# Moving the first-product weights of an MLP to another place in SBUF

## The chip, the cores and the metric

The kernel runs on one core of a Trainium2 chip. The metric is the device time of one execution in microseconds (us), as the median of several runs. The core has a matrix engine (TensorE, PE in the profile, with its weight loads under PEld), VectorE (DVE), ScalarE (ACT), GpSimd (POOL) and SyncE (SP, which here issues DMAs). Its on-chip memory SBUF has 128 partitions; every tensor there has a start, given below in bytes of a partition.

## The reference

Two transformer layers run on 1024 tokens of width 1024 and, in the first layer, 256 context tokens as well. Everything is float32. Each layer modulates its input, runs an attention mixer (the first layer's has a spatial-gating branch beside it), adds, normalises, and then runs the MLP:

```python
x = _layer_norm(ALPHA * x + g_m * _squared_relu_mlp(x * (1 + sc_m) + sh_m, mlp_w1[l], mlp_w2[l]), ...)

def _squared_relu_mlp(h, w1, w2):          # h: tokens x 1024, w1: 1024 x 4096, w2: 4096 x 1024
    return jnp.square(jax.nn.relu(h @ w1)) @ w2
```

The first layer's MLP has 1280 rows (tokens and context), the second's 1024.

## The kernel before

The program is a chain of stages (the list at the end of `build`), each a block of five engine programs. Engines meet at the end of a block, and inside one they are ordered only by semaphores written out by hand. No planner or allocator chooses anything: the order of the instructions is the source's, and every SBUF tensor is placed at an explicit start. `Place` hands out starts one behind the other.

Precision is kept by splitting each float32 operand into a high and a low part (names that end in `h` and `l`), each of a type that TensorE takes as it is. Each product is then three matmuls: high by high, high by low, low by high. The call is `pe.matmul(out, weights, streamed)`: the second argument is loaded into the array (a LDWEIGHTS in the trace), the third is streamed past it. In the profile's names, `pair<-hth,m_wah` streams `hth` past the weights `m_wah`.

`hth` and `htl` are the modulated columns: the layer's input, turned so that features lie on partitions, with 1280 tokens for each of 8 feature tiles. They start at byte 20608 and end at byte 102528, called `after_ht`. Before the change the sums `y` (10 tiles of 1024 elements) start there, `moments` lie behind them, and `after_y` is 143584. The MLP stage and the row stages of kind 2 place all their tensors from `after_y`; the other stages place theirs from `after_ht`, over `y`.

`stage_mlp` (L1251 to L1438) goes over the 4096 hidden features in NCH = 16 steps of 256, that is M = 2 tiles of 128. For each step:

- SP loads `rawa` (a piece of w1) and `rawb` (a piece of w2).
- ACT copies `rawa` to `wah` (L1323) and POOL subtracts to get `wal` (L1346), two tiles of 128x1024 each; ACT and DVE do the same for `wbh` and `wbl`.
- PE runs the first product (L1434 to L1436) for each group of 512 tokens (the first layer has a third group of 256), for each of the two hidden tiles and 8 feature tiles, three matmuls each: 48 matmuls for a group. The weights are `wah` and `wal`; the streamed operands are `hth` and `htl`.
- ACT takes the relu and the square to `ath`, POOL squares to `sq`, and DVE subtracts to get `atl`.
- PE runs the second product (L1418 to L1420) of the step before, 12 matmuls for each tile of 128 tokens, with weights `ath` and `atl` and streamed `wbh` and `wbl`. It stands ahead of the first product of the same group, so runs of the two products alternate.
- DVE adds the result to `y` (L1368).

The attention stage has a projection loop, `job` (L1163 to L1165), with the same triple in the same form: the same `hth` and `htl`, in the same groups of 512 and 256 tokens and the same 8 feature tiles, past the weights `a_wkh`, `a_wqh`, `a_wvh` and their low parts. It also differs in the start of the weights, the PSUM banks used, the number of feature tiles run without a break, and what runs around it. The gating stage (L709 to L711) has the roles turned: its weights are `hth` and `htl`, and it streams `gate_wh` and `gate_wl`.

Starts before the change, in bytes, with the remainder after division by 128 (worked out from the source):

| tensors | role | start | remainder |
|---|---|---|---|
| hth, htl | streamed in the first product | 20608, 61568 | 0 |
| m_wah, m_wal | weights of the first product | 143584, 151776 | 96 |
| m_wbh, m_wbl | streamed in the second product | 159968, 168160 | 96 |
| m_ath, m_atl (layer 0; 1) | weights of the second product | 192736, 202976; 192736, 200928 | 96 |
| a_wkh, a_wqh, a_wvh | weights in attention | 114816, 118912, 123008 | 0 |
| a_wkl, a_wql, a_wvl | weights in attention | 127104, 131200, 135296 | 0 |
| gate_wh, gate_wl | streamed in the gating stage | 102528, 135296 | 0 |
| y, moments | DVE's sums | 102528, 143488 | 0 |

All steps inside these tensors are multiples of 128 bytes.

Of the kernel before, what the change touches and what calls it, by code (L numbers as in the profile page):

```python
# [13 lines left out]
F32 = mybir.dt.float32  # L14
F32R = mybir.dt.float32r
# [4 lines left out]
P = 128  # L20
D = 1024
KT = D // P
SEQ, CTX = 1024, 256
TOK = SEQ + CTX
XT, CT = SEQ // P, CTX // P
# [3 lines left out]
FC = 256  # L29
# [1222 lines left out]
def stage_mlp(nc, io, k, layer):  # L1252
# [6 lines left out]
    tag = f"m{layer}"  # L1259
    sb = Place(nc, tag, k.after_y)  # L1260
    tiles = XT + CT if layer == 0 else XT
    groups = groups_of(tiles * P)
    NG, M = len(groups), FC // P
    J = NG * M
    NB1 = 3 if J % 3 == 0 else 4
    wah, wal = sb("wah", [P, M, KT, P], F32R), sb("wal", [P, M, KT, P], F32R)
    wbh, wbl = sb("wbh", [P, M, D], F32R), sb("wbl", [P, M, D], F32R)
    rawa, rawb = sb("rawa", [P, M, KT, P]), sb("rawb", [P, M, D])
    ath, atl = sb("ath", [P, M, tiles * P], F32R), sb("atl", [P, M, tiles * P], F32R)
# [197 lines left out]
def build(nc, io, out):  # L1467
    k = Kept(nc)
    k.out = out
    at = 16512  # L1470
    small = {}
    for name, shape in (("ident", [P, P]), ("eps", [P, 1]), ("mod", [P, 2, 48, 2])):
        small[name] = nc.alloc_sbuf_tensor_at(f"kept_{name}", shape, F32, offset=at)
        at += (int(np.prod(shape[1:])) * 4 + 31) // 32 * 32
    assert at <= BASE
    k.ident, k.eps, k.mod = (small[x] for x in ("ident", "eps", "mod"))
    k.hth = nc.alloc_sbuf_tensor_at("hth", [P, KT, TOK], F32R, offset=BASE)
    k.htl = nc.alloc_sbuf_tensor_at("htl", [P, KT, TOK], F32R, offset=BASE + KT * TOK * 4)
    k.after_ht = BASE + 2 * KT * TOK * 4
    k.y = nc.alloc_sbuf_tensor_at("y", [P, XT + CT, D], F32, offset=k.after_ht)  # L1480
    k.mv = nc.alloc_sbuf_tensor_at("moments", [P, XT + CT, 2], F32, offset=k.after_ht + (XT + CT) * D * 4)
    k.after_y = k.after_ht + (XT + CT) * D * 4 + 96
    assert (XT + CT) * 2 * 4 <= 96
    pairs = [nc.alloc_psum_tensor(f"pair{i}", [P, 1024], F32) for i in range(4)]
    k.pair = pairs
    k.bank = [pairs[i // 2][:, (i % 2) * 512:(i % 2) * 512 + 512] for i in range(8)]
    k.x_dram = nc.dram_tensor("x_rows", [TOK, D], F32, kind="Internal").ap()
    k.cat_dram = nc.dram_tensor("cat_cols", [D, TOK], F32, kind="Internal").ap()
    k.gate_dram = nc.dram_tensor("gate_rows", [2, 2, 2 * KT, P], F32, kind="Internal").ap()
    k.skew_dram = nc.dram_tensor("skewed_rpb", [16, P, GRID_R * RP_W], F32, kind="Internal").ap()  # L1490
    k.rp_dram = nc.dram_tensor("padded_rpb", [16, RP_W, RP_W], F32, kind="Internal").ap()
    stages = [(stage_modulation, ()), (stage_rows, (0, 0)), (stage_attention, (0,)), (stage_gating, ()), (stage_rows, (0, 1)),
              (stage_mlp, (0,)), (stage_rows, (0, 2)),
              (stage_attention, (1,)), (stage_rows, (1, 1)), (stage_mlp, (1,)), (stage_rows, (1, 2))]
    for stage, args in stages:
        stage(nc, io, k, *args)
        k.end_stage()
# [22 lines left out]
```

## Time and profile before

| | us |
|---|---|
| median of 3 runs | 3334.58 (3331.59 to 3334.59) |
| profiled execution, its own time | 3334.39 |
| its span, first to last instruction | 3332.6 |
| PE busy in the span | 2858.8 (86%) |
| MLP of layer 0, first matmul to last run's end | 875.85 to 1770.99 |
| MLP of layer 1 | 2567.08 to 3279.92 |

The profile records one execution. A matmul's recorded duration overlaps the next one's, since they are pipelined, so what a matmul costs is the distance from its start to the start of the next. The timeline gives starts to 0.01 us; over a run of n matmuls the distance is the difference of two starts divided by n. PEclk is the granted TensorE clock as a share of 2.4 GHz.

### The profile page before, as it was taken

To read this page: it belongs to the slowest core of one execution; us is meant where nothing else is said; L and a number is where in the kernel's file an instruction comes from. 1 tells how busy PE (TensorE), PEld (TensorE's weight loads), DVE (VectorE), ACT (ScalarE), POOL (GpSimd) and SP (SyncE) were. 2 spreads that over 40 slices of the span, in tenths; PEclk is the share of its full clock that TensorE was granted. 3 is DMA by queue.
4 is the path that set the end of the run, shared out by engine and by line. 5 is a ranking of instruction groups with operands and counts; after the bars stand their busy time and mean duration, and the time that the engine had idled before them with its cause. 6 is when DMAs were issued, how large, how long until landed. Compare 5 with 4: busy or idle time off the path is not lost. (4 is left out here: it accounts for less than half of the span.)

```text
span 3332.6 us, 40345 instructions
## 1 busy us (share of the span) xinstructions
PE 2858.8 (86%) x15572; PEld 2328.3 (70%) x15572; DVE 1392.0 (42%) x2191; ACT 886.1 (27%) x1664; POOL 557.6 (17%) x377
## 2 busy tenths in 40 slices
PE   3477776869799999999994799999877999999993
PEld 0166665748588888888883688888665888888882
DVE  1156563136433333333338355555554333333336
ACT  0133333324312121212113344334333221122111
POOL 0000000113312121212126100000013222221124
PEclk8778788979899999999996899999988999999997
DMA  9721002034201010101013211110053111111114
GB/s 366 284 81 29 21 21 72 19 120 133 85 29 47 29 48 27 49 27 49 27 38 114 81 45 39 33 45 20 7 171 101 51 50 50 50 44 44 50 38 114
DMA packets 201373, 228.92 MB, mean 69 GB/s; under 512 B 15000, under 2 KB 148720, under 8 KB 201264
## 3 DMA queue, kind: packets, MB, share of 16 engines
q1 hardware_dynamic: 200800, 227.19, 21.8%
q8 instruction: 74, 1.21, 0.1%
q14 instruction: 35, 0.29, 0.0%
q10 hardware_dynamic: 464, 0.23, 0.0%
HBM read 198.98 MB, written 32.63 MB: 70 GB/s over the span
## 5 line engine op out<-in xcount | busy, mean ns | idle before, releaser
L1434 PE MATMUL pair<-hth,m_wah 128*128 128x512 f32 (+1 forms) x1280 | 480.1, 375 | 27.8 <-POOL m_wal L1346 27.8
L1368 DVE TENSOR_TENSOR y<-y,pair 128x1024 f32<-128x1024 f32 x288 | 351.2, 1220 | 337.4 <-PE pair L1420 337.2
L1435 PE MATMUL pair<-htl,m_wah 128*128 128x512 f32 (+1 forms) x1280 | 480.0, 375 | 0.0
L1436 PE MATMUL pair<-hth,m_wal 128*128 128x512 f32 (+1 forms) x1280 | 479.5, 375 | 0.0
L1418 PE MATMUL pair<-m_wbh,m_ath 128*128 128x512 f32 x1152 | 449.2, 390 | 4.6 <-DVE y L1368 4.6
L1420 PE MATMUL pair<-m_wbh,m_atl 128*128 128x512 f32 x1152 | 449.5, 390 | 0.0
L1419 PE MATMUL pair<-m_wbl,m_ath 128*128 128x512 f32 x1152 | 449.4, 390 | 0.0
L1396 DVE TENSOR_TENSOR m_atl<-m_sq,m_ath 128x512 fp32r<-128x512 f32 x160 | 102.2, 639 | 715.5 <-POOL m_sq L1353 715.5
L1336 ACT ACTIVATE m_rel<-pair 128x512 f32<-128x512 f32 x160 | 88.7, 554 | 1037.2 <-PE pair L1436 1037.2
L1353 POOL TENSOR_TENSOR m_sq<-m_rel 128x512 f32<-128x512 f32 x160 | 154.5, 965 | 1231.3 <-ACT m_rel L1336 1231.3
L1434 PEld LDWEIGHTS pair<-hth,m_wah 128*128 128x128 f32 x1280 | 242.4, 189 | 76.1 <-POOL m_wal L1346 28.6
L1436 PEld LDWEIGHTS pair<-hth,m_wal 128*128 128x128 f32 x1280 | 242.5, 189 | 47.4
L1435 PEld LDWEIGHTS pair<-htl,m_wah 128*128 128x128 f32 x1280 | 242.2, 189 | 47.3
L1418 PEld LDWEIGHTS pair<-m_wbh,m_ath 128*128 128x128 f32 x1152 | 216.3, 188 | 53.4 <-DVE y L1368 7.6
L1419 PEld LDWEIGHTS pair<-m_wbl,m_ath 128*128 128x128 f32 x1152 | 216.2, 188 | 46.1
L1420 PEld LDWEIGHTS pair<-m_wbh,m_atl 128*128 128x128 f32 x1152 | 216.2, 188 | 45.5
L982 ACT ACTIVATE a_sx<-a_sx,a_small 128x640 f32<-128x640 f32 (+4 forms) x208 | 160.8, 774 | 179.6 <-DVE a_small L1084 179.6
L1218 PE MATMUL pair<-a_ptt,a_v 128*64 128x128 f32 x1888 | 138.3, 296 | 72.6 <-ACT a_ptt L989 68.7
L1218 PEld LDWEIGHTS pair<-a_ptt,a_v 128*64 128x64 f32 x1888 | 111.2, 146 | 103.1 <-ACT a_ptt L989 81.9
L1346 POOL TENSOR_TENSOR m_wal<-m_rawa,m_wah 128x1024 fp32r<-128x1024 f32 x64 | 152.6, 2406 | 49.8 <-ACT m_wah L1323 49.8
L381 ACT ACTIVATE r_modt<-pair,kept_mod 128x128 f32<-128x128 f32 x304 | 109.1, 529 | 183.4 <-PE pair L523 171.4
L538 PE MATMUL pair<-r_wh,r_cath 128*128 128x512 f32 x288 | 117.7, 409 | 38.9 <-DVE r_wl L443 22.6
(171 smaller groups left out, 4460.6 us busy)
## 6 DMA issues: line engine op xcount, KB each, us to landing
mod_w<-in_w_mod SPq DMA_DIRECT2D x24, 2048.0 KB, 20.0
m_rawa<-in_mlp_w SPq DMA_DIRECT2D x64, 512.0 KB, 4.2
m_rawb<-in_mlp_w SPq DMA_DIRECT2D x64, 512.0 KB, 4.2
x_rows<-r_res SPq DMA_DIRECT2D x28, 512.0 KB, 3.1
r_raw<-cat_cols SPq DMA_DIRECT2D x18, 512.0 KB, 5.9
m_rawa<-x_rows SPq DMA_DIRECT2D x18, 512.0 KB, 3.8
r_xin<-in_x SPq DMA_DIRECT2D x16, 512.0 KB, 3.9
skewed_rpb<-padded_rpb SPq DMA_DIRECT2D x8, 512.0 KB, 6.4
```

The costliest lines, as they stand in the source:

```text
L538: pe.matmul(o, cath[:, t % 2, kt, :], wh[:, kt, n], start=kt == 0, stop=False)
L982: act.activation(x, x, ACT.Exp, bias=sm[:, 0:1], scale=-1.0, accum_out=sm[:, 1:2]).then_inc(s_exp, 1)
L1218: i = pe.matmul(TA[ds, 0:P], v[:, it % KB, kt, ds], ptt[:, hh, j, :], start=j == 0, stop=j == len(tiles) - 1)
L1346: pool.tensor_tensor(wal[:, m, :, :], rawa[:, m, :, :], f32(wah[:, m, :, :]), ALU.subtract).then_inc(s_alow, 1)
L1353: pool.tensor_tensor(sq[:, m % 2, 0:n], r, r, ALU.mult).then_inc(s_sq, 1)
L1368: dve.tensor_tensor(k.y[:, t, :], k.y[:, t, :], k.pair[t % 2][:, :], ALU.add).then_inc(s_y, 1)
L1418: pe.matmul(o, ath[:, m, ts], wbh[:, m, cols], start=m == 0, stop=False)
L1419: pe.matmul(o, ath[:, m, ts], wbl[:, m, cols], start=False, stop=False)
L1420: i = pe.matmul(o, atl[:, m, ts], wbh[:, m, cols], start=False, stop=m == M - 1)
L1434: pe.matmul(o, wah[:, m, kt, :], xh, start=kt == 0, stop=False)
L1435: pe.matmul(o, wah[:, m, kt, :], xl, start=False, stop=False)
L1436: i = pe.matmul(o, wal[:, m, kt, :], xh, start=False, stop=kt == KT - 1)
```

## The change

`wah` and `wal` are placed from `after_ht`, directly behind `htl`, by a placer of their own. `y` and `moments` start 16 KB (16384 bytes) further on, behind them, and so does everything that is placed from `after_y`. In the MLP stage the two tensors that left that sequence were 16 KB together, so all other MLP tensors keep their starts. The row stages of kind 2 move their tensors by 16 KB. No instruction, loop, wait or transfer is added, removed or put in another place.

```diff
@@ stage_mlp
-    wah, wal = sb("wah", [P, M, KT, P], F32R), sb("wal", [P, M, KT, P], F32R)
+    near = Place(nc, f"{tag}n", k.after_ht)
+    wah, wal = near("wah", [P, M, KT, P], F32R), near("wal", [P, M, KT, P], F32R)
+    assert near.at <= k.y_at
     wbh, wbl = sb("wbh", [P, M, D], F32R), sb("wbl", [P, M, D], F32R)
@@ build
     k.after_ht = BASE + 2 * KT * TOK * 4
-    k.y = nc.alloc_sbuf_tensor_at("y", [P, XT + CT, D], F32, offset=k.after_ht)
-    k.mv = nc.alloc_sbuf_tensor_at("moments", [P, XT + CT, 2], F32, offset=k.after_ht + (XT + CT) * D * 4)
-    k.after_y = k.after_ht + (XT + CT) * D * 4 + 96
+    k.y_at = k.after_ht + 2 * FC * KT * 4
+    k.y = nc.alloc_sbuf_tensor_at("y", [P, XT + CT, D], F32, offset=k.y_at)
+    k.mv = nc.alloc_sbuf_tensor_at("moments", [P, XT + CT, 2], F32, offset=k.y_at + (XT + CT) * D * 4)
+    k.after_y = k.y_at + (XT + CT) * D * 4 + 96
```

| tensors | start before | start after | remainder by 128 before, after |
|---|---|---|---|
| m_wah, m_wal | 143584, 151776 | 102528, 110720 | 96, 0 |
| y, moments | 102528, 143488 | 118912, 159872 | 0, 0 |
| row stages of kind 2, first tensor | 143584 | 159968 | 96, 96 |
| other MLP tensors | 159968 and on | the same | 96, 96 |

## Rows read from the trace of the kernel before

**Rows 1.** The page: the span, and PE's busy time, share and instructions.

```profile
span 3332.6 us, 40345 instructions
PE 2858.8 (86%) x15572; PEld 2328.3 (70%) x15572; DVE 1392.0 (42%) x2191; ACT 886.1 (27%) x1664; POOL 557.6 (17%) x377
```

**Rows 2.** Busy time by stretch: the two MLP stages; the first line names the columns.

```profile
core 0: us, PE busy (x) PEld busy (x) DVE busy (x) ACT busy (x) POOL busy (x), PEclk, DMA share, GB/s
875.85:1770.99 895.14, 892.02 (x4223) 742.38 (x4224) 307.16 (x317) 166.28 (x254) 185.66 (x135) 1.00 0.13 41
2567.08:3279.92 712.84, 711.34 (x3069) 578.46 (x3070) 246.17 (x240) 139.31 (x190) 157.53 (x101) 1.00 0.17 49
```

**Rows 3.** Waits of PE (us in total, times, longest), windows 870:1740 and 2600:3290.

```profile
PE pair L1434 <- POOL m_wal L1346: 13.4, 1, 13.4
PE pair L1418 <- DVE y L1368: 1.5, 2, 0.8
```

**Rows 4.** Groups by line and form: busy us, mean ns of one, idle before.

```profile
L1418 PE MATMUL pair<-m_wbh,m_ath 128*128 128x512 f32 x1152 | 449.2, 390 | 4.6 <-DVE y L1368 4.6
L1434 PE MATMUL pair<-hth,m_wah 128*128 128x512 f32 x1024 | 408.3, 399 | 27.8 <-POOL m_wal L1346 27.8
...
L1346 POOL TENSOR_TENSOR m_wal<-m_rawa,m_wah 128x1024 fp32r<-128x1024 f32 x64 | 152.6, 2406 | 49.8 <-ACT m_wah L1323 49.8
...
L1434 PE MATMUL pair<-hth,m_wah 128*128 128x256 f32 x256 | 71.9, 281 | 0.0
```

**Rows 5.** PE's timeline, layer 0's MLP: start us, duration us, instruction.

```profile
1106.49 0.40 PE L1434 MATMUL pair<-hth,m_wah 128*128 128x512 f32 x1
...
1117.73 0.39 PE L1418 MATMUL pair<-m_wbh,m_ath 128*128 128x512 f32 x1
...
1119.82 0.39 PE L1418 MATMUL pair<-m_wbh,m_ath 128*128 128x512 f32 x1
...
1123.22 0.28 PE L1434 MATMUL pair<-hth,m_wah 128*128 128x256 f32 x1
...
1128.92 0.40 PE L1418 MATMUL pair<-m_wbh,m_ath 128*128 128x512 f32 x1
...
1129.62 0.39 PE L1418 MATMUL pair<-m_wbh,m_ath 128*128 128x512 f32 x1
...
1139.82 0.40 PE L1434 MATMUL pair<-hth,m_wah 128*128 128x512 f32 x1
```

**Rows 6.** The same view, layer 1's MLP.

```profile
2779.96 0.40 PE L1434 MATMUL pair<-hth,m_wah 128*128 128x512 f32 x1
...
2791.20 0.39 PE L1418 MATMUL pair<-m_wbh,m_ath 128*128 128x512 f32 x1
```

**Rows 7.** The same view, layer 0's attention projections.

```profile
208.08 0.28 PE L1163 MATMUL pair<-hth,a_wkh 128*128 128x256 f32 x1
...
210.96 0.40 PE L1163 MATMUL pair<-hth,a_wqh 128*128 128x512 f32 x1
...
212.12 0.39 PE L1165 MATMUL pair<-hth,a_wql 128*128 128x512 f32 x1
...
230.20 0.39 PE L1163 MATMUL pair<-hth,a_wvh 128*128 128x512 f32 x1
...
235.64 0.28 PE L1163 MATMUL pair<-hth,a_wvh 128*128 128x256 f32 x1
```

**Rows 8.** The same view, the gating stage.

```profile
549.65 0.39 PE L709 MATMUL pair<-gate_wh,hth 128*128 128x512 f32 x1
...
550.33 0.39 PE L709 MATMUL pair<-gate_wh,hth 128*128 128x512 f32 x1
```

**Rows 9.** The same view, the start of layer 0's MLP.

```profile
881.14 0.63 PE L1434 MATMUL pair<-hth,m_wah 128*128 128x512 f32 x1
881.57 0.63 PE L1435 MATMUL pair<-htl,m_wah 128*128 128x512 f32 x1
```

**Rows 10.** The instructions that use y: duration min/median/max in ns.

```profile
L1368 DVE TENSOR_TENSOR y<-y,pair x288: 1172/1221/1223, 909.9 to 3284.1; 128x1024 f32<-128x1024 f32 x144
```

## The prediction

> **What bounds the kernel now.** I read the page first: the span is 3332.6 us and PE is busy for 86% of it [rows 1]. The busy time by stretch then shows where PE is the limit. In the two MLP stages it is busy for 892.02 of 895.14 us and 711.34 of 712.84 us, at the full granted clock, while DVE, POOL and ACT are busy for about a third of the time or less [rows 2]. The waits confirm it: in nearly all of layer 0's MLP PE waits once, 13.4 us for the first step's m_wal, and in layer 1's it waits 1.5 us for y [rows 3]. So these 1608 us, almost half of the span, last as long as PE's instructions take one after another. What a matmul costs there reaches the end of the kernel whole.
>
> The groups by form give the first hint: a 512-column matmul of the first product is recorded with 399 ns, one of the second product with 390 ns [rows 4]. Durations overlap, so I went to the timeline and divided differences of starts.
>
> - First product, layer 0: 48 matmuls from 1106.49 to 1117.73 us, 11.24 / 48 = 234.2 ns each [rows 5].
> - First product, layer 1: 48 from 2779.96 to 2791.20, again 234.2 ns [rows 6].
> - Second product: 45 from 1129.62 to 1139.82, 10.20 / 45 = 226.7 ns [rows 5].
> - Attention projections: 24 from 230.20 to 235.64, 5.44 / 24 = 226.7 ns [rows 7].
> - Gating: 3 from 549.65 to 550.33, 226.7 ns [rows 8].
>
> So the first product's matmuls, 47% of the 512-column ones in the MLP, cost 7.5 ns more than the others, with the same number of columns and at the same clock. The reader should see that the attention projection is the same triple over the same hth and htl with the same groups and feature tiles. It runs at 226.7. Of the differences between the two loops the source leaves the weights' place, the PSUM bank and the neighbours. Other PE work runs before and after both, and the second product, which shares the MLP's neighbours, is quick.
>
> **What the place could have to do with it.** No row gives an address, so this is inference from the source's starts. It is not distance and not a region: hth's and htl's feature tiles begin up to 122,976 bytes ahead of m_wah and end 41,056 ahead of it, and attention's weights begin 12,288 to 114,688 bytes behind them, an overlapping stretch, and the gating stage streams gate_wl through the very bytes in which m_wah and m_wal lie, at 226.7 [rows 8]. What separates the slow pair from every fast pair is the remainder by 128: weights at 96 and streamed operand at 0, where attention and gating have 0 and 0 and the second product has 96 and 96. After the change the first product has 0 and 0, and its weights lie in the area in which attention's do. That they would then behave as attention's is my forecast.
>
> **Term 1, the 512-column matmuls of the first product.** There are 16 steps x 2 groups x 2 hidden tiles x 8 feature tiles x 3 = 1536 per layer, 3072 in all; the form's count of 1024 for one of the three lines agrees [rows 4]. At the start of each MLP stage the granted clock is low for some dozen matmuls and the distance there is 0.43 us (881.14 to 881.57), which is 512 columns at 1.2 GHz with nothing on top [rows 9]. I leave 24 of them out: 3048 x 7.5 ns = 22.9 us. All of it is on the path.
>
> **Term 2, the switches between the products.** After a run of the first product the second takes nine matmuls to settle: 1117.73 to 1119.82 is 2.09 us where nine at 226.7 would be 2.04 [rows 5]. Attention's five matmuls after its switch from 256 to 512 columns take 1.16 us instead of 1.13 [rows 7]. There are 64 switches from a 512-column run into the second product (2 groups x 16 steps x 2 layers). If both runs keep one beat these 0.05 us vanish, -3.2 us. If instead each switch into the first product gains such a tail too, since one operand family is at remainder 0 and the other at 96, it is +3.2 us. No row shows a switch between two quick pairs of different remainders, so both stay as bounds; I take 0, the middle, since nothing is nearer to either.
>
> **Term 3, the 256-column matmuls.** In the MLP 48 take 1123.22 to 1128.92, 118.8 ns each [rows 5]; in attention 24 take 208.08 to 210.96, 120.0 ns [rows 7]. Here the present place is the better one. There are 3 x 256 = 768 [rows 4]: 768 x 1.2 = +0.9 us.
>
> **Term 4, y and the rest.** y's start keeps remainder 0 and the row stages' tensors keep 96. The 288 additions into y, which lie in up to ten different places, take 1172 to 1223 ns with a median of 1221 [rows 10], so a place 16 KB further on has no price that this view shows. In the loop each addition is also hidden by the 12 matmuls of the next tile (12 x 0.227 = 2.72 us against 1.22); without that cover it would cost PE the difference to 2.72. At the ends of the stages, where it is not hidden, the whole spread over 18 tiles is 18 x 0.05 = 0.9 us either way. I take 0. Writing wah and wal is ACT's and POOL's work, 2.4 us for a tile on POOL [rows 4]. It starts when a step's first product ends and is wanted after 48 matmuls of the second (10.9 us): two tiles and ACT's copies fit. If the cover were gone PE would wait as at the first step [rows 3]. SP's queue and all transfers are as before, and rawa does not move.
>
> **A rule that speaks against it.** The Trainium skill, SBUF — State Buffer, "Who interferes with whom", gives PE two SBUF read ports, one for the streamed operand and one for weights, calls them independent, and says that PE never waits on anyone. By it the weights' place could not matter, and the sum would be 0. The trace shows 234.2 against 226.7 for the same triple [rows 5 to 7], which that rule leaves unexplained; no row shows the cause.
>
> **Sum.** -22.9 + 0 + 0.9 + 0 = -22.0 us. The profiled execution took 3334.4 us, 1.8 more than its span, and this lies around the instructions and stays. That gives 3312.4; the median of the runs is 3334.6, 0.2 higher, so 3312.6.
>
> **Rivals.**
>
> 1. *Nothing changes* (12%). The 7.5 ns come from something other than the place: the banks, the neighbours, or how the loop is fed. The page's independent ports say the same. For it: only one slow pair exists in the trace, and no view names a cause. Against it: attention's loop issues the same instructions over the same columns at 226.7 [rows 7], and the second product has the same neighbours at 226.7 [rows 5]. Time: 3334.6.
>
> 2. *Only one of the two weight tensors becomes quick* (6%). wah feeds two matmuls of each triple and wal one. If the distance from the streamed rows matters as well as the remainder, one of them could stay slow. For: they lie 8 KB apart. Against: hth's and htl's different distances make no difference today. Gain a third or two thirds of 22.9, less 0.9: 3334.6 - 6.7 = 3327.9 or 3334.6 - 14.4 = 3320.2.
>
> 3. *Both products become slow* (3%). The second product today finds its beat again within nine matmuls after each switch. With two quick families of different remainders it may lose it at each switch, and the first may not gain it. The price would be 3456 x 7.5 = +25.9 us on the second product (3 x 1152 [rows 4]) with term 1 gone: 3360. It decides against the change once the mean distance over all 6504 of them is above today's (3048 x 234.2 + 3456 x 227.7) / 6504 = 230.7 ns, where 227.7 is the second product with its tail, (2.09 + 39 x 0.2267) / 48 us. Against: attention's switches settle in five matmuls [rows 7].
>
> **How the numbers follow.** My forecast has 79%. Its own range is the bounds of terms 2 and 4 (4.1 us) and the runs' scatter of up to 3 us below the median: 3306 to 3318. The range for 8 in 10 reaches into the second rival: 3306 to 3328; no change and slower (15%) and a few per cent of the rest stay out. What a measurement can tell from no change is about 0.2%, 6.7 us, so faster means below 3327.9. Faster: 79 + 5 = 84%. Same: 12 + 1 = 13%. Slower: 3%.
>
> **What would show it.** In the timeline after, 48 matmuls of the first product should take 10.88 us instead of 11.24, and a 256-column run 5.76 instead of 5.70. L1434's mean at 512 columns should fall from 399 to about 391 ns, and L1418's should stay near 390. PE's waits should stay as they are, and the two MLP stages should shrink by about 11 us each (layer 0 some 0.9 less, for the 256-column runs). Term 2 shows in the nine matmuls after each switch, on both sides. The prediction is wrong if the 48 still take 11.24 us, if a new wait stands in front of L1434, or if the second product's run leaves 226.7.

## The result, and the profile after

The changed kernel takes 3316.9 us (median of 5 runs, 3313.9 to 3322.1) against 3334.6 for the kernel before (3331.6 to 3338.0): a ratio of 0.995 with a 95% interval of 0.9938 to 0.9962. The gain is 17.7 us where 22.0 were forecast. The profiled execution took 3320.6 us, with a span of 3318.8 against 3332.6 [rows 1]. One run of e9_far_same_512 below, 3542.7 us at a mean granted clock of 0.80 where every other run had 0.92 or 0.93, is left out of its time.

The busy time of the two MLP stages after the change has the columns of rows 2 (layer 1's window ends 0.46 us ahead of its last matmul's start):

```profile
880.68:1766.92 886.24, 882.92 (x4224) 741.83 (x4224) 307.29 (x317) 166.48 (x254) 185.07 (x135) 1.00 0.13 41
2563.26:3266.50 703.24, 701.75 (x3069) 577.69 (x3070) 246.08 (x239) 139.33 (x190) 157.55 (x101) 1.00 0.17 50
```

From the first matmul's start to the last's, layer 0's MLP went from 895.14 to 886.24 us and layer 1's from 713.30 (2567.08 to 3280.38) to 703.70 (2563.26 to 3266.96): 8.9 + 9.6 = 18.5 us less. Instruction counts, busy DVE and the granted clock are as they were. PE's waits are the same ones too, as in rows 3 but for the line numbers and the name of one tile:

```profile
PE pair L1436 <- POOL m0n_wal L1348: 13.4, 1, 13.4
```

```profile
PE pair L1420 <- DVE y L1370: 1.5, 2, 0.8
```

The groups by form, which answer to rows 4 (the first product's are now split by layer, since its weights have a name for each):

```profile
L1420 PE MATMUL pair<-m_wbh,m_ath 128*128 128x512 f32 x1152 | 449.8, 390 | 4.8 <-DVE y L1370 4.8
...
L1436 PE MATMUL pair<-hth,m0n_wah 128*128 128x512 f32 x512 | 200.3, 391 | 13.4 <-POOL m0n_wal L1348 13.4
L1436 PE MATMUL pair<-hth,m1n_wah 128*128 128x512 f32 x512 | 200.3, 391 | 14.6 <-POOL m1n_wal L1348 14.6
...
L1436 PE MATMUL pair<-hth,m0n_wah 128*128 128x256 f32 x256 | 72.3, 283 | 0.0
```

The reader sees 399 ns gone to 391 at 512 columns and 281 gone to 283 at 256. The timeline of PE at the step of rows 5:

```profile
1108.27 0.39 PE L1436 MATMUL pair<-hth,m0n_wah 128*128 128x512 f32 x1
...
1119.19 0.40 PE L1420 MATMUL pair<-m_wbh,m_ath 128*128 128x512 f32 x1
...
1121.28 0.39 PE L1420 MATMUL pair<-m_wbh,m_ath 128*128 128x512 f32 x1
...
1124.69 0.28 PE L1436 MATMUL pair<-hth,m0n_wah 128*128 128x256 f32 x1
...
1130.44 0.40 PE L1420 MATMUL pair<-m_wbh,m_ath 128*128 128x512 f32 x1
...
1141.38 0.39 PE L1436 MATMUL pair<-hth,m0n_wah 128*128 128x512 f32 x1
```

The 48 matmuls of the first product last 10.92 us instead of 11.24, 227.5 ns each. The 256-column run lasts 1124.69 to 1130.44, 5.75 us instead of 5.70. A run of the second product behind it lasts 10.94 us, where it was 1128.92 to 1139.82, 10.90 [rows 5]. Additions into y keep their durations [rows 10]:

```profile
L1370 DVE TENSOR_TENSOR y<-y,pair x288: 1172/1221/1222, 913.5 to 3270.7; 128x1024 f32<-128x1024 f32 x144
```

The table gives the mean distance over all starts of a trace. Only distances under 400 ns are taken, which leaves out the low clock and the waits. It shows where the time went:

| | before | after | difference |
|---|---|---|---|
| first product, 512 columns, some 3050 | 234.27 ns | 227.60 ns | -20.3 us |
| first product, 256 columns, 768 | 118.76 ns | 119.75 ns | +0.8 us |
| second product, 3447 | 227.81 ns | 228.25 ns | +1.5 us |

That is -18.0 of the 18.5 us.

### The profile page after: what moved, and what is told of

Read it like the earlier page. It is cut to its first block and busy times, and to the rows that moved or that the text cites. A ratio compares the mean times of both kernels' runs of the same rounds, so it can differ in the third digit from the quotient of the medians.

```text
span 3318.8 us, 40345 instructions
## 1 busy us (share of the span) xinstructions
PE 2840.9 (86%) x15572; PEld 2328.4 (70%) x15572; DVE 1392.2 (42%) x2191; ACT 886.3 (27%) x1664; POOL 557.1 (17%) x377
## 5 line engine op out<-in xcount | busy, mean ns | idle before, releaser
L1436 PE MATMUL pair<-hth,m0n_wah 128*128 128x512 f32 (+1 forms) x768 | 272.6, 355 | 13.4 <-POOL m0n_wal L1348 13.4
L1437 PE MATMUL pair<-htl,m0n_wah 128*128 128x512 f32 (+1 forms) x768 | 273.0, 355 | 0.0
L1438 PE MATMUL pair<-hth,m0n_wal 128*128 128x512 f32 (+1 forms) x768 | 272.9, 355 | 0.0
L1436 PE MATMUL pair<-hth,m1n_wah 128*128 128x512 f32 x512 | 200.3, 391 | 14.6 <-POOL m1n_wal L1348 14.6
L1437 PE MATMUL pair<-htl,m1n_wah 128*128 128x512 f32 x512 | 200.7, 392 | 0.0
L1438 PE MATMUL pair<-hth,m1n_wal 128*128 128x512 f32 x512 | 200.6, 392 | 0.0
L1436 PEld LDWEIGHTS pair<-hth,m0n_wah 128*128 128x128 f32 x768 | 145.6, 190 | 35.0 <-POOL m0n_wal L1348 13.8
L1437 PEld LDWEIGHTS pair<-htl,m0n_wah 128*128 128x128 f32 x768 | 145.6, 190 | 21.8
L1438 PEld LDWEIGHTS pair<-hth,m0n_wal 128*128 128x128 f32 x768 | 145.7, 190 | 20.3
```

The source lines that it names most:

```text
L1436: pe.matmul(o, wah[:, m, kt, :], xh, start=kt == 0, stop=False)
L1437: pe.matmul(o, wah[:, m, kt, :], xl, start=False, stop=False)
L1438: i = pe.matmul(o, wal[:, m, kt, :], xh, start=False, stop=kt == KT - 1)
```

## The experiments

Three questions were put to the chip: is it the place or the remainder, which remainder, and what are the slow matmuls that follow a switch from one product to the other (the "tail"). "Far" means that wah and wal lie behind y, as before the change, "near" that they lie directly behind the columns. A family is the set of operands of one product; two products are in one family when all their operands have the same remainder. All distances are read as above, from the run of the first product near 1100 us of the layer 0 MLP unless told otherwise; means are over all starts.

**Wah and wal where they were, with remainder 0 by 128.**

```diff
+    sb.at += 32
     wah, wal = sb("wah", [P, M, KT, P], F32R), sb("wal", [P, M, KT, P], F32R)
+    sb.at += 96
```

> The kernel before with wah and wal 32 bytes further on, so that they start at 143616 and 151808 (remainder 0 by 128), nothing else of the MLP changed in its remainder. Remainder theory (weights and streamed operand need the same remainder by 128): the first product's 512-column matmuls go from 234.3 to about 227.6 ns, the 256-column ones from 118.8 to 119.8, the kernel to about 3317 us. Place theory (weights must lie near the columns): 234.3 ns and 3334.6 us as before. If the remainder by 512 counts instead of that by 128, it stays slow too, because hth has 128 and wah 256.

```profile
1104.02 0.40 PE L1436 MATMUL pair<-hth,m_wah 128*128 128x512 f32 x1
...
1115.22 0.39 PE L1420 MATMUL pair<-m_wbh,m_ath 128*128 128x512 f32 x1
```

Measured: 11.20 / 48 = 233.3 ns, a mean of 233.40, and 3328.0 us (ratio 0.9989, 0.998 to 0.9999). My remainder by 128 is refuted. Place and a coarser remainder are both left.

**Wah and wal near, with remainder 96.**

```diff
-    near = Place(nc, f"{tag}n", k.after_ht)
+    near = Place(nc, f"{tag}n", k.after_ht + 96)
-    k.y_at = k.after_ht + 2 * FC * KT * 4
+    k.y_at = k.after_ht + 2 * FC * KT * 4 + 128
```

> The changed kernel with wah and wal 96 bytes further on (102624 and 110816, remainder 96), still directly behind the columns; y moves 128 bytes with them and keeps remainder 0. Remainder theory: the first product is back at 234.3 ns and the kernel at about 3334 us. Place theory: it stays at 227.6 ns and 3317 us.

```profile
1106.11 0.40 PE L1436 MATMUL pair<-hth,m0n_wah 128*128 128x512 f32 x1
...
1117.35 0.39 PE L1420 MATMUL pair<-m_wbh,m_ath 128*128 128x512 f32 x1
```

Measured: 234.2 ns again, mean 234.13, 3331.2 us (ratio 0.9996, 0.9984 to 1.0008). Being near does not suffice: 96 bytes take the whole gain away.

**All MLP tensors at remainder 0 by 128, far and near.** The first is the kernel before, the second the changed kernel, each with `after_y` 32 bytes further on:

```diff
-    k.after_y = k.after_ht + (XT + CT) * D * 4 + 96
+    k.after_y = k.after_ht + (XT + CT) * D * 4 + 128
```
```diff
-    k.after_y = k.y_at + (XT + CT) * D * 4 + 96
+    k.after_y = k.y_at + (XT + CT) * D * 4 + 128
```

> The kernel before with after_y 32 bytes further on: every MLP tensor and every tensor of the row stages of kind 2 has remainder 0, wah and wal stay far from the columns. Remainder theory: both products at 226.7 ns. Tail theory A (the slow matmuls after each switch between the products come from the change of remainder 0 to 96 and back): they go, the means of both fall to about 226.9 ns, the kernel to 3334.6 - 22.5 - 3.1 + 0.8 = 3310 us. Tail theory B (any switch of operands costs them): means of 227.6 and 228.2, 3317 us. Place theory: 3334.6 us.

> The changed kernel with after_y 32 bytes further on, so that the second product's operands and the row stages have remainder 0 as well. Tail theory A: 3310 us, means of 226.9 ns in both products. Tail theory B: 3317 us, as the changed kernel. Against e5_far_all_0 it differs only in the place of wah and wal: remainder theory says the same time within 2 us.

```profile
1106.35 0.40 PE L1434 MATMUL pair<-hth,m_wah 128*128 128x512 f32 x1
...
1117.54 0.39 PE L1418 MATMUL pair<-m_wbh,m_ath 128*128 128x512 f32 x1
```

```profile
1103.67 0.39 PE L1436 MATMUL pair<-hth,m0n_wah 128*128 128x512 f32 x1
...
1114.56 0.39 PE L1420 MATMUL pair<-m_wbh,m_ath 128*128 128x512 f32 x1
```

Far (first fence): 11.19 us, mean 233.18 ns, 3327.3 us (ratio 0.9991, 0.9981 to 1.0001); the remainder theory as I had it is wrong here as well. Near (second fence): 10.89 us, means of 226.94 and 227.27 ns, 3308.4 us (ratio 0.993, 0.9914 to 0.9947). In the near one tail theory A holds in direction: the slow matmuls after a switch are nearly gone, and its two MLP stages together take 1584.9 us where the changed kernel's take 1589.9. Between the two the remainders by 256 of wah less hth differ, 128 and 0, as well as the place.

**Far, with hth's remainder by 512, and far, 256 off it.**

```diff
+    sb.at += 416
     wah, wal = sb("wah", [P, M, KT, P], F32R), sb("wal", [P, M, KT, P], F32R)
+    sb.at += 96
```
```diff
+    sb.at += 160
     wah, wal = sb("wah", [P, M, KT, P], F32R), sb("wal", [P, M, KT, P], F32R)
+    sb.at += 352
```

> The kernel before with wah and wal 416 bytes further on, at 144000 and 152192: far from the columns, remainder 128 by 512 as hth and htl have; the second product's operands are 512 bytes further on and keep their remainders. Remainder-by-512 theory (the pair needs the same remainder by 512; equal by 128 is not enough): the first product runs at 227.6 ns as in the changed kernel and the kernel is 18 us faster than before, about 3315 us. Place theory (near the columns): it stays above 233 ns and the kernel within 5 us of before.

> As e9_far_same_512, but wah and wal at 143744 and 151936, 256 bytes off hth's remainder by 512. If the remainder by 256 is what counts: 227.6 ns. If that by 512: above 231 ns. Place theory: above 233 ns.

```profile
1102.58 0.39 PE L1436 MATMUL pair<-hth,m_wah 128*128 128x512 f32 x1
...
1113.50 0.40 PE L1420 MATMUL pair<-m_wbh,m_ath 128*128 128x512 f32 x1
```

```profile
1104.03 0.39 PE L1436 MATMUL pair<-hth,m_wah 128*128 128x512 f32 x1
...
1114.95 0.40 PE L1420 MATMUL pair<-m_wbh,m_ath 128*128 128x512 f32 x1
```

Both last 10.92 us, exactly the changed kernel's run; the means are 227.51 and 227.56 ns. The first took 3312.3 us (median of three; ratio 0.9931, 0.991 to 0.9952), the second, a single run, 3313.2. With this the place is out: wah and wal lie 41 KB behind the columns with y between, and the whole gain is there. And equality by 256 bytes is enough; by 512 it is not needed.

**Near, 128 off.** The counterpart:

```diff
-    near = Place(nc, f"{tag}n", k.after_ht)
+    near = Place(nc, f"{tag}n", k.after_ht + 128)
-    k.y_at = k.after_ht + 2 * FC * KT * 4
+    k.y_at = k.after_ht + 2 * FC * KT * 4 + 512
```

> The changed kernel with wah and wal 128 bytes further on (102656 and 110848): still directly behind the columns, same remainder by 128 as hth, but 128 off by 512. y and all behind it move by 512 bytes and keep their remainders. Remainder-by-512 theory: the same slow pattern as e1_weights_0, 233.4 ns. Place theory: 227.6 ns.

```profile
1109.22 0.39 PE L1436 MATMUL pair<-hth,m0n_wah 128*128 128x512 f32 x1
...
1120.38 0.40 PE L1420 MATMUL pair<-m_wbh,m_ath 128*128 128x512 f32 x1
```

11.16 / 48 = 232.5 ns, mean 232.55; a single run of 3331.5 us. Slow as the theory says, though 0.9 ns quicker than e1_weights_0, with which it shares the offset: how slow an unequal pair is does not hang on the offset alone.

**Another offset.** `sb.at += 64` ahead of wah and `sb.at += 64` behind wal, in the kernel before.

> The kernel before with wah and wal 64 bytes further on, at 143648 and 151840, 160 off hth's remainder by 256 (before: 96 off, 234.3 ns; e1_weights_0: 128 off, 233.4 ns). Remainder-by-256 theory: still slow, between 231 and 236 ns; if it only matters that they are equal, no finer order of the offsets is expected. Whole time within 5 us of before.

```profile
1103.48 0.39 PE L1436 MATMUL pair<-hth,m_wah 128*128 128x512 f32 x1
...
1114.67 0.39 PE L1420 MATMUL pair<-m_wbh,m_ath 128*128 128x512 f32 x1
```

Measured: 11.19 us, a mean of 233.25 ns; 3327.3 us in a single run. Slow, as expected.

**Both products in one family.**

```diff
-    k.after_y = k.y_at + (XT + CT) * D * 4 + 96
+    k.after_y = k.y_at + (XT + CT) * D * 4 + 512
```

> The changed kernel with after_y at 160384: the second product's operands and the row stages' tensors have remainder 128 by 512, as the first product's. If the slow matmuls after a switch come from the change of remainder between the products, they go now altogether: means of 226.7 ns in both products, 1 to 3 us under e6_near_all_0 (where the remainders by 512 are 128 and 256), about 3306 us. If they come from the switch itself: as e6_near_all_0.

```profile
1091.59 0.39 PE L1420 MATMUL pair<-m_wbh,m_ath 128*128 128x512 f32 x1
...
1102.47 0.39 PE L1436 MATMUL pair<-hth,m0n_wah 128*128 128x512 f32 x1
...
1113.35 0.39 PE L1420 MATMUL pair<-m_wbh,m_ath 128*128 128x512 f32 x1
```

A run of the second product and one of the first last 10.88 us each, 226.7 ns from the first matmul to the last: no slow matmul follows a switch. The means are 226.70 and 227.11 ns. Most of what is left in the second stands behind the 256-column runs; no remainder changes there, so its cause is another one, which no run separates (attention shows a tail behind its 256-column matmuls too [rows 7]). The kernel takes 3307.2 us, a ratio of 0.9922 (0.9904 to 0.9939), the quickest of all: 27 us below the kernel before in the same set of runs (3334.0), 10 below the changed one's median, of which the MLP stages' traces show 6.8. The two MLP stages, in the view of rows 2:

```profile
875.65:1758.30 882.65, 879.54 (x4223) 741.92 (x4224) 307.08 (x317) 166.38 (x254) 185.20 (x135) 1.00 0.13 41
2551.99:3252.43 700.44, 698.98 (x3072) 577.85 (x3072) 246.86 (x242) 139.29 (x190) 157.81 (x101) 1.00 0.17 50
```

**The same family, at another remainder.** The kernel above with `BASE = 20704`, so that all of it but the kept tensors moves by 96 bytes.

> As e11_one_family with the columns and everything placed behind them 96 bytes further on: hth and htl at 20704 and 61664, wah and wal at 102624 and 110816, all with remainder 224 by 256 where they had 128. If only the equality of the remainders counts: means of 226.7 ns in both products and the time of e11_one_family, 3307 us within 3. If the remainder itself matters as well, the distances rise above 227 ns.

```profile
1106.86 0.39 PE L1436 MATMUL pair<-hth,m0n_wah 128*128 128x512 f32 x1
...
1117.73 0.39 PE L1420 MATMUL pair<-m_wbh,m_ath 128*128 128x512 f32 x1
```

10.87 us, means of 226.72 and 227.09 ns; the MLP stages last 882.8 and 700.3 us, as in e11_one_family. At these two values, 128 and 224, only the equality counts and not the remainder itself. Its time, 3310.8 us (ratio 0.9927, 0.9907 to 0.9947), missed my 3 us by half a microsecond. In its trace the difference lies outside the MLP, in the two attention stages (325.0 and 570.4 us against 320.8 and 566.7, first projection to last product); see the next section.

**The second product's weights 32 bytes off.** The changed kernel with one line more:

```diff
+    sb.at += 32
     ath, atl = sb("ath", [P, M, tiles * P], F32R), sb("atl", [P, M, tiles * P], F32R)
```

> The changed kernel with ath and atl (and what lies behind them) 32 bytes further on: the second product's weights are 32 off its streamed wbh and wbl by 256, where they were equal. Remainder-by-256 theory, for any pair of weights and streamed operand: the second product goes from 228.2 to between 232 and 235 ns, 14 to 23 us more on 3447 matmuls, 3331 to 3340 us against the changed kernel's 3317; the first product stays at 227 to 228 ns. If only the first product's operands (or the columns' own start) matter: 228.2 ns and 3317 us.

```profile
1091.64 0.39 PE L1421 MATMUL pair<-m_wbh,m_ath 128*128 128x512 f32 x1
...
1102.83 0.39 PE L1437 MATMUL pair<-hth,m0n_wah 128*128 128x512 f32 x1
...
1113.74 0.39 PE L1421 MATMUL pair<-m_wbh,m_ath 128*128 128x512 f32 x1
```

Now the second product is the slow one: 11.19 / 48 = 233.1 ns, mean 233.37, and the first stays quick with 10.91 us. In the MLP stages that is 16.0 us more than in the changed kernel (895.0 + 710.9 against 886.2 + 703.7). The single run's 3327.8 us is below the 3331 to 3340 I gave; its first attention stage lasted 321.3 us where the changed kernel's profiled one lasted 324.9.

**Attention 96 bytes off.** The changed kernel with `sb.at += 96` ahead of all tensors of both attention stages.

> The changed kernel with all tensors of both attention stages 96 bytes further on, so that the projections' weights are 96 off hth's remainder by 256, as the MLP's first product was before. Remainder-by-256 theory: in the unbroken projections at the start of the first attention stage the distance goes from 226.7 to about 234.3 ns; the whole kernel gains some 0.0075 x 960 = 7 us at most, less where PE waits for others. If the slow pair had something of the MLP's own as its cause: 226.7 ns.

```profile
226.95 0.40 PE L1164 MATMUL pair<-hth,a_wvh 128*128 128x512 f32 x1
...
238.19 0.28 PE L1164 MATMUL pair<-hth,a_wvh 128*128 128x256 f32 x1
```

The 48 projections last 11.24 us, 234.2 ns, the kernel before's first product to the hundredth; before, this loop ran at 226.7 [rows 7]. So the slow distance is nothing of the MLP's own. The single run took 3322.4 us.

All together, by weights' start less streamed operand's start, after division by 256:

| offset | pair and kernel | mean ns at 512 columns |
|---|---|---|
| 0 | first, e11_one_family and e14_one_family_224 | 226.7 |
| 0 | first, e6_near_all_0 (second product's operands 128 further by 256) | 226.9 |
| 0 | first, after, e9, e10, e7 and e13 (second product at another remainder) | 227.4 to 227.6 |
| 0 | second, all but e7 | 227.1 to 228.3 |
| 32 | second, e7_second_mixed | 233.4 |
| 96 | first, before and e2_near_96 | 234.3, 234.1 |
| 96 | attention's 48 projections, e13_attention_off_96 | 234.2 |
| 128 | first, e1_weights_0, e5_far_all_0, e12_near_off_128 | 233.4, 233.2, 232.6 |
| 160 | first, e3_weights_32 | 233.3 |

The offsets 64, 192 and 224 were not run.

## Why the prediction was right, and where not

The time lay in the range, 4.3 us above the forecast, and the way to it mostly held. The range needs a word: with terms 2 and 4 at their dear bounds the sum gives 3316.7 us, so the measured 3316.9 lies at the edge of what the sum allowed; the room above it, up to 3328, was there for the runs' scatter and rival 2.

*What bounds the kernel* held: with no wait changed and no instruction changed, the MLP stages shrank by what their matmuls' distance shrank by.

*What the place could have to do with it* was right in its choice and wrong in its number. It is the remainder and not nearness or a region: e2_near_96 loses the gain near, e9_far_same_512 has it far. But equality by 128 bytes is not enough; by 256 it is. Every pair that rows 5 to 8 show was either equal by 256 or 96 off, so they could not tell 64, 128, 256 or 512 apart; I took 128, without having a row for it. It did no harm to the forecast because the change makes wah and hth equal by 256 too (both 128), and that was luck. It would have cost most of the gain, had I used it to lay out a kernel: e1_weights_0, e5_far_all_0 and e12_near_off_128 are equal by 128 and slow, and their MLP stages gain 4.5, 3.7 and 6.0 us where the change gains 18.5.

*Term 1* was -22.9 us. The steady distance is 226.7 as forecast; the tails, which I had set apart in term 2, make the mean 227.6 and leave -20.3.

*Term 2* is the step that failed in size. I took 0 with bounds of 3.2 us either way. Measured: (227.60 - 226.67) x 3050 = +2.8 us in the first product and +1.5 in the second, together +4.3, outside the bounds. I had reckoned with a new tail into the first product, and it is there; I had not reckoned that the second product's would grow. It did behind the 256-column runs (10.90 to 10.94 us each, 0.6 us in all) and behind the 512-column runs (0.9 us in all). That a change of family brings these tails, the reason I gave for the dear bound, is what e11_one_family shows: in one family they are gone at the switches between 512-column runs, another 6.8 us of MLP time (1589.9 to 1583.1). Not every change of family costs as much. In e6_near_all_0 the two products are 128 apart by 256, and 5.0 of the 6.8 us are there. In e3_weights_32 the first product's weights, its columns and the second product's operands have three different remainders (32, 128 and 224), and the second product's mean is 227.11 ns, as in one family. What sets the size of a tail stays open.

*Term 3* was +0.9 and is +0.8. *Term 4* was 0; the additions into y show none. The sum of the steps as measured is -18.0, and the stages give -18.5.

*The rest of the kernel* I took as fixed. It is not quite: the first attention stage lasts between 320.4 and 326.6 us in profiles of kernels in which not an instruction of it differs (e9_far_same_512 and e12_near_off_128), and took 3.3 us more in the changed kernel's profile than in the one before; the second lasts between 566.3 and 570.8 us (e9_far_same_512 and e2_near_96). That is most of why the profiled difference (13.8 us) is smaller than the MLP's, and why single runs here say little below 5 us. The medians' 17.7 us agree with the MLP's 18.5.

*The rule that spoke against it.* The Trainium skill, SBUF — State Buffer, "Who interferes with whom", calls PE's two SBUF read ports independent; taken to mean that the weights' place cannot matter, it would have given no change. The runs contradict that reading in two loops: 96 bytes in the weights' start make the loop slow in attention (226.7 to 234.2) and in the MLP (227.6 in the changed kernel, 234.1 in e2_near_96). For this kernel the measurement decides: the place of the two operands relative to each other costs 3% of a matmul's time.

Rival 1 is out. Rival 2 is out: wah and wal, at one remainder, became quick together. Rival 3, both products slow, did not come; its mechanism, a beat lost at each switch, exists, but the beat is found again within a dozen matmuls.

## What to carry to other kernels

Where TensorE is the limit, take the distance of starts, not the recorded duration, and compare loops of one form; a constant few ns more in one of them is worth a search. Lay out the weights and the streamed operand of a product so that their starts have the same remainder by 256 bytes, and give products that alternate the same remainder; here the two together gave 27 us of 3334. Padding alone gave the first part, 512 bytes in all in e9_far_same_512. When a rule is inferred from one slow pair, try its counterexamples before using it: equality by 128 bytes fitted every pair of rows 5 to 8, and was not enough.

## What the runs showed of the hardware

In these loops, in which every matmul has 128x128 weights loaded for it, a matmul of 512 columns settles at a distance of 226.7 ns at the full clock when the two operands' starts are equal by 256 bytes. The mean is 232.6 to 234.3 when they are 32, 96, 128 or 160 off. At a granted clock of 0.50, which is 1.2 GHz, the distance is 0.43 us for the pair 96 off (881.14 to 881.57 [rows 9]) and the same for the equal one, as the changed kernel's start of layer 0's MLP shows:

```profile
882.12 0.63 PE L1436 MATMUL pair<-hth,m0n_wah 128*128 128x512 f32 x1
882.55 0.63 PE L1437 MATMUL pair<-htl,m0n_wah 128*128 128x512 f32 x1
882.98 0.63 PE L1438 MATMUL pair<-hth,m0n_wal 128*128 128x512 f32 x1
```

The steps of both alternate between 426 and 427 ns. So the price of being 96 off exists at the full clock alone. At 256 columns in the MLP it does not exist either: the means are 117.6 to 119.8 ns unequal, 119.8 to 119.9 equal. The unequal distances are not noise but a figure that repeats (231, 234, 235, 233, 232, 237, 238 ns at 96 off, the same within 1 ns in the MLP before and in e13_attention_off_96), while equal pairs settle within a dozen matmuls to 227, 227, 226. What in the chip makes this figure stays open: no run here looks inside the two reads.
